# Routed experts on one core: the four with the fewest tokens in half the places, large and small alternating

## The chip, the core and the metric

One core of a Trainium2 chip runs the whole program: two blocks of a first kind, then two of a second. The time is device microseconds of that core, from launch to end; a profiled execution gives the span from the first to the last instruction. TensorE (PE) multiplies, VectorE (DVE) and ScalarE (ACT) work on SBUF and PSUM, SyncE (SP) issues the transfers. PEld is the loading of a stationary matrix into TensorE.

## The reference

The layer that the change touches routes each of 256 tokens of width 1024 to two of eight experts; the expert's inner width is 3584. The program computes the same sum, but each expert only over the tokens that chose it.

```python
def moe_swiglu(h, w_router, b_router, w_gate, w_up, w_down):
    t = h.reshape(B * S, D)
    logits = (t @ w_router).astype(jnp.float32) + b_router.astype(jnp.float32)
    top_v, top_i = lax.top_k(logits, TOP_K)
    top_w = jax.nn.softmax(top_v, axis=-1)
    gates = jnp.sum(jax.nn.one_hot(top_i, N_EXPERTS, dtype=jnp.float32) * top_w[..., None], axis=1)
    out = jnp.zeros_like(t)
    for e in range(N_EXPERTS):
        out = out + gates[:, e:e + 1].astype(t.dtype) * swiglu(t, w_gate[e], w_up[e], w_down[e])
    return out.reshape(B, S, D)
```

## The kernel before

All weights are float32 in memory and come in units of 128 x 2048 (1 MB), one transfer each, into four raw buffers. To multiply at float32 accuracy with TensorE's faster rounded type (float32r), every operand is cut into a high part, which is the value rounded, and a low part, which is what the rounding left. ScalarE makes the high part of a unit (`split_hi`, L549 to L553), VectorE the low part (`split_lo`, L1056 to L1059); each has three buffers. A product is then three matmuls: high by high, high by low, low by high (`mm3`, L1796, on L1789). SP loads a raw buffer again when the low part taken from it is done (`load`, L494 to L501), ScalarE writes a high buffer again when TensorE has used the unit in it. `take` on each engine moves this stream on by one unit; ScalarE and VectorE split two units ahead.

The router (L1463 on VectorE, L2216 on TensorE) computes the logits, marks for each token its two best experts (`rank`), counts on TensorE which place each token gets in its expert (`slots`), and the largest count (`most`). Every expert has 128 places. `routed` (L840, L1505, L2267) gathers the tokens of all experts with matmuls by one-hot matrices, four experts and one of eight pieces of the width in each of 16 steps. ScalarE copies the high rows out (`xghi`), VectorE the low ones (`xglo`). Between the router's steps TensorE runs matmuls of ones on nothing, so that it isn't idle (`keep_warm`, L1791).

An expert is cut into seven groups of 512 inner columns. A group is six units: two for gate, two for up (`up`, L2314 on TensorE, L854 on ScalarE, L1554 on VectorE) and two for down (`down`, L2335, L864, L1571). The tokens are the stationary operand, 512 weight columns move. A unit is 12 matmuls of 512 columns. After gate and up, ScalarE takes silu (L860), VectorE multiplies it by the up result and the token's gate (`mact`, L1565), TensorE turns the result round in four transposes (L2310), and the two engines split it again (`mahi`, `malo`, L882 and L1590). The 56 groups run expert by expert, `down` of a group behind `up` of the next. An expert's output stays in two PSUM banks over its seven groups, is split (`ohi`, `olo`), and goes back to the tokens by scatter matmuls in four pieces (`expert_to_x`, L2302), which VectorE adds to the residual stream `xT` (L1550). The order of the 336 units in memory and in time is `MOE_ORDER`, a constant.

If one expert has more than 128 tokens, a flag makes a second, unpipelined round run over all weights (`over_round`). In the profiled run it doesn't run.

Of the kernel before, what the change touches and what calls it, by code (L numbers as in the profile page):

```python
# [56 lines left out]
PER_G = 6  # L57
U_MOE = PER_G * NG
# [3 lines left out]
MOE_ORDER = [0, 1, 2, 3]  # L62
# [62 lines left out]
def build(nc, io):  # L125
    ctx = ExitStack()
    with ctx:
# [54 lines left out]
        half_out = sem("expert_half_out")  # L182
        lam_dotted, lam_exped = sem("lam_dotted"), sem("lam_exped")
# [45 lines left out]
        mahi_end = rt.put("mahi_end", [P, GF // P, P], F32R)  # L229
        malo_end = rt.put("malo_end", [P, GF // P, P], F32R)  # L230
# [6 lines left out]
        vx = base.put("vx", [P, 8 + 64 + 8 + 64])  # L237
# [6 lines left out]
        small = base.put("small", [P, 512])  # L244
        stat = base.put("stat", [P, PB, 8])
        overflow = base.put("overflow", [1, 1], mybir.dt.int32)
        rstd = base.put("rstd", [P, S])
# [15 lines left out]
        iota = c1.put("iota", [P, P])  # L263
        at_moe = c1.top + -c1.top % 256
# [70 lines left out]
        gs1 = rm.put("gs1", [P, 1])  # L335
        r = Region(at_places)
        ohi = r.put("ohi", [P, D], F32R)
        olo = r.put("olo", [P, D], F32R)
        rows_hi_T = at("rows_hi_T", [P, NT, D], at_hhi, F32R)
# [52 lines left out]
        def moe_act(n):  # L392
            return (mahi_end, malo_end) if n == NG - 1 else (mahi, malo)
# [99 lines left out]
        def sync_program(sp):  # L493
            def load(s):  # L494
# [15 lines left out]
            for name, t in (("onehot", onehot_in), ("lbw", lbw), ("ident", ident), ("bsum", bsum),  # L510
                            ("lmask", lmask), ("halves", halves), ("tri", tri), ("future", future_in), ("v2", v2), ("vx", vx),
                            ("iota", iota)):
                sp.dma_start(t[:], io[name]).then_inc(small_loaded, 16)
            for s in range(4, U_SECOND + RAW):
                load(s)
            sp.wait_ge(expert_added, 4 * NE)
            flag = sp.value_load(overflow[0:1, 0:1], min_val=0, max_val=1)
            with sp.If(flag > 0):
                for r in range(1, ROUNDS):
                    with sp.Fori(0, NE) as e:  # L520
                        for i in range(PER_G * GE):
                            n = (r - 1) * U_MOE + i
                            sp.wait_ge(over_used, e * (PER_G * GE) + (n + 1))
                            sp.dma_start(slow_raw[:], io["wm"][bass.ds(e * (PER_G * GE) + i, 1), :, :].rearrange(
# [11 lines left out]
        def scalar_program(act):  # L536
# [18 lines left out]
            def take():  # L555

                s = stream.next() - 1
                if s + LEAD < U_ALL:
                    split_hi(s + LEAD)
# [280 lines left out]
            def routed(r):  # L840
                for i in range(16):
                    es, k, b = slice(4 * (i // DK), 4 * (i // DK) + 4), i % DK, i % 4 * 2
                    after(gathered_hi)
                    act.activation(xghi[:, es, k, :], PS[:, b, :].rearrange("p (e s) -> p e s", e=4),
                                   ACT.Copy).then_inc(taken_act, 1)
                after(places_turned)
# [6 lines left out]
            def experts():  # L853
                def up(n):  # L854
                    take()
# [3 lines left out]
                    act.wait_ge(unit_used, used)  # L859
                    act.activation(msil[:], PS[:, 2 + 2 * (n % 2), :], ACT.Silu).then_inc(moe_silu, 1)  # L860
                    take()
                    take()

                def down(n):  # L864
                    take()
                    if n == NG - 1:
                        after(half_out)
                        act.activation(ohi[:, 0:512], PS[:, 0, :], ACT.Copy).then_inc(out_hi, 1)
                        act.wait_ge(unit_used, stream.n + 1)
                        act.activation(ohi[:, 512:], PS[:, 1, :], ACT.Copy).then_inc(out_hi, 1)  # L870
                        take()
                        return
                    if n == NG - 2:
                        turn(n + 1)
                    used = take()
                    if n % GE == GE - 1:
                        act.wait_ge(unit_used, used)
                        act.activation(ohi[:], banks(0, 2), ACT.Copy).then_inc(out_hi, 1)

                def turn(n):  # L880
                    after(moe_turned)
                    act.activation(moe_act(n)[0][:].rearrange("p f s -> p (f s)"), PS[:, 6, :],  # L882
                                   ACT.Copy).then_inc(moe_hi, 1)

                up(0)
                for n in range(1, NG):
                    up(n)
                    down(n - 1)
                    if n < NG - 1:
                        turn(n)  # L890
                down(NG - 1)
# [151 lines left out]
        def vector_program(dve):  # L1043
# [17 lines left out]
            def take():  # L1061

                s = stream.next() - 1
                if s + LEAD < U_ALL:
# [196 lines left out]
            def first_mixer(l):  # L1261
# [6 lines left out]
                if l == 0:  # L1268
                    after(small_loaded, 16 * 11)
                    dve.tensor_copy(future[:], future_in[:].unsqueeze(1).to_broadcast([P, 2, P]))  # L1270
                    dve.tensor_copy(ident_r[:], ident[:])
                    dve.memset(nd[:].bitcast(F32), 0.0)
# [188 lines left out]
            eq = small[:, 192:320].rearrange("p (t e j) -> p t e j", t=NT, e=NE)  # L1461

            def router():  # L1463
# [22 lines left out]
                token_rows(0)  # L1486
                after(slots_done)
                cnt = PS[:, 3, 0:NT * NE].rearrange("p (t e) -> p t e", t=NT)
                dve.tensor_tensor(slots.rearrange("p (t e) -> p t e", t=NT), cnt, rank, ALU.mult).then_inc(slots_shifted, 1)
                after(slots_shifted)  # L1490

            def gating():
# [5 lines left out]
                step(dve.tensor_tensor(ex, ex, m.unsqueeze(2).to_broadcast([P, NT, NE]), ALU.mult))  # L1498
                halves = idg[:, :, P:TG].rearrange("p t (e h) -> p t e h", h=2)
                step(dve.tensor_copy(halves[:, :, :, 0], ex))  # L1500
                dve.tensor_copy(idg[:, :, 0:P], ident[:].unsqueeze(1).to_broadcast([P, NT, P]))
                dve.tensor_tensor(halves[:, :, :, 1], ex, halves[:, :, :, 0].bitcast(F32),
                                  ALU.subtract).then_inc(gates_ready, 1)

            def routed(r):  # L1505
                sl = small[:, 416:432] if r else slots
                if r:
                    dve.tensor_scalar(sl, slots, float(-P * r), None, ALU.add).then_inc(slots_shifted, 1)
                    after(slots_shifted)

                def place(es):
                    shape = [P, NT, NE // 2, P]
                    slot_of = sl.rearrange("p (t e) -> p t e", t=NT)[:, :, es]
                    dve.tensor_tensor(places[:, :, es, :], iota[:].unsqueeze(1).unsqueeze(1).to_broadcast(shape),
# [3 lines left out]
                if r == 0:  # L1518
                    after(totals_done)
                    dve.tensor_reduce(most, PS[0:1, 1, 32:32 + NE], AX, ALU.max).then_inc(slots_ready, 1)  # L1520
                    after(slots_ready)
                    token_rows(1)
                for i in range(16):
# [24 lines left out]
            def expert_to_x(e, q, bank=None):  # L1548
                after(scattered)
                dve.tensor_tensor(pair(xT, q), pair(xT, q), PS[:, bank or 6 + q % 2, :],  # L1550
                                  ALU.add).then_inc(expert_added, 1)

            def experts():
                def up(n):  # L1554
                    e = n // GE
                    for i in range(4):
                        if n == 1 and i == 2:
                            turn(0)
                        if n % GE == 2 and n > GE and 1 <= i <= 2:
                            expert_to_x(e - 1, 1 + i)  # L1560
                        if n or i < 3:
                            used = take()
                    after(moe_silu)
                    dve.wait_ge(unit_used, used + (n == 0))
                    dve.scalar_tensor_tensor(out=mact[:], in0=msil[:], scalar=gsl[:, e:e + 1],  # L1565
                                             in1=PS[:, 3 + 2 * (n % 2), :], op0=ALU.mult,
                                             op1=ALU.mult).then_inc(moe_mult, 1)
# [3 lines left out]
                def down(n):  # L1571
                    take()
                    if n == NG - 2:
                        turn(n + 1)
                    if n < NG - 1:
                        take()
                    if n == NG - 1:
                        for c in range(2):
                            cs = slice(c * 512, (c + 1) * 512)
                            after(out_hi)  # L1580
                            dve.tensor_tensor(olo[:, cs], PS[:, c, :], ohi[:, cs].bitcast(F32),
                                              ALU.subtract).then_inc(out_lo, 1)
                    elif n % GE == GE - 1:
                        after(out_hi)
                        dve.tensor_tensor(olo[:], banks(0, 2), ohi[:].bitcast(F32), ALU.subtract).then_inc(out_lo, 1)

                def turn(n):
                    hi, lo = (x[:].rearrange("p f s -> p (f s)") for x in moe_act(n))
                    after(moe_hi)
                    dve.tensor_tensor(lo, PS[:, 6, :], hi.bitcast(F32), ALU.subtract).then_inc(moe_lo, 1)  # L1590

                up(0)
                for n in range(1, NG):
                    up(n)
                    if n % GE == 1 and n > 1:
                        expert_to_x(n // GE - 1, 0)
                        expert_to_x(n // GE - 1, 1)
                    down(n - 1)
                    if n < NG - 1:
                        turn(n)  # L1600
                down(NG - 1)
                for q in range(4):
                    expert_to_x(NE - 1, q, (6, 7, 2, 3)[q])
# [165 lines left out]
        def tensor_program(pe):  # L1769
# [314 lines left out]
            def first_mixer(l):  # L2084
# [3 lines left out]
                if l == 0:  # L2088
                    after(small_loaded, 16 * 11)
# [126 lines left out]
            def router():  # L2216
# [34 lines left out]
                keep_warm(0, 12)  # L2251
# [442 lines left out]
```

## Time and profile before

| | us |
|---|---|
| median of three runs | 2510.22 |
| lowest, highest | 2506.88, 2510.34 |
| the profiled execution: its own time | 2507.98 |
| the profiled execution: span | 2506.2 |
| expert stage, first to last expert matmul | 586.2 to 1566.0 |

In the rows below, times are us from the start of the span unless marked ns. In the table of stretches a row has the stretch and its length, then for each engine (PE, PEld, DVE, ACT, POOL) its busy time and, in brackets, its instructions; then come the granted TensorE clock as a share of 2.4 GHz, the busy share of the 16 transfer engines, and the rate. Matmul ends are modelled and matmuls overlap, so the step from one to the next counts, not the duration.

### The profile page before, as it was taken

How to read it: one execution, taken by the hardware profiler on the slowest of the kernel's cores; microseconds unless marked ns; L12 is line 12 of the kernel's file. 1: busy time of each engine (PE TensorE's matmuls, PEld its weight loads, DVE VectorE, ACT ScalarE, POOL GpSimd, SP SyncE). 2: the span in 40 equal slices, each digit the busy share in tenths (PEclk: the TensorE clock that was granted, in tenths of full speed). 3: DMA queues.
4: the chain of work that ended last, by engine and by line, in shares of the span. 5: the costliest groups of instructions: out<-in, count | busy, mean ns of one | idle time of the engine just before them, and what ended most of it. 6: DMA issues, size and time to landing. Idle time of an engine off the chain costs nothing.

```text
span 2506.2 us, 38463 instructions
## 1 busy us (share of the span) xinstructions
PE 2463.3 (98%) x16646; PEld 2220.8 (89%) x16646; DVE 1863.2 (74%) x1635; ACT 1520.1 (61%) x1558; POOL 0.2 (0%) x4
## 2 busy tenths in 40 slices
PE   9999999999999999999999999999999999999998
PEld 8899999887888888888888888998999999899998
DVE  6765557858888889888888888756875565767655
ACT  6563436567777777777777777557653365665433
POOL 0000000000000000000000000000000000000000
PEclk9999999999999999999999999999999999999999
DMA  6335554325999999999999999433444543343552
GB/s 250 135 120 185 184 187 150 135 85 207 369 350 366 357 365 359 363 361 365 353 359 353 368 356 367 168 135 118 152 166 175 198 167 138 118 168 135 186 185 85
DMA packets 83314, 585.25 MB, mean 234 GB/s; under 512 B 9245, under 2 KB 11133, under 8 KB 12613
## 3 DMA queue, kind: packets, MB, share of 16 engines
q1 hardware_dynamic: 83140, 582.73, 62.8%
q8 instruction: 135, 2.21, 0.4%
q14 instruction: 39, 0.31, 0.0%
HBM read 581.64 MB, written 1.05 MB: 232 GB/s over the span
## 4 chain that ended last, share of the span: by engine, by line
PE 85%; DVE 7%; ACT 4%; DMA 2%; issue 1%; DVEq 0%; SPq 0%; ACTq 0%
PE PS L1789 84%; DVE wlo L1058 3%; ACT whi L553 2%; DMA raw<-in_wm 2%; PE PS L2310 1%; PE PS L1993 1%; DVE stat L1190 0%; ACT pb L666 0%; DVE hT L1104 0%; ACT pt L681 0%; DVE lf L1244 0%; DVE pb L1215 0%; DMA xT<-in_xT 0%; DVE xT L1363 0%; DVE yT L1249 0%
## 5 line engine op out<-in xcount | busy, mean ns | idle before, releaser
L1058 DVE TENSOR_TENSOR wlo<-raw,whi 128x2048 fp32r<-128x2048 f32 x550 | 1257.9, 2291 | 376.3 <-ACT whi L553 368.5
L553 ACT ACTIVATE whi<-raw 128x2048 fp32r<-128x2048 f32 x550 | 1051.6, 1913 | 322.0 <-PE PS L1789 289.0
L1789 PE MATMUL PS<-hhi,whi 128*128 128x256 f32 x1984 | 569.7, 287 | 6.3 <-DVE wlo L1058 1.7
L1789 PE MATMUL PS<-hhi,wlo 128*128 128x256 f32 x1984 | 558.2, 281 | 0.0
L1789 PE MATMUL PS<-hlo,whi 128*128 128x256 f32 x1984 | 558.0, 281 | 0.0
L1789 PEld LDWEIGHTS PS<-hhi,whi 128*128 128x128 f32 x1984 | 373.4, 188 | 16.8 <-issue 12.0
L1789 PEld LDWEIGHTS PS<-hlo,whi 128*128 128x128 f32 x1984 | 373.6, 188 | 1.0 <-issue 0.5
L1789 PEld LDWEIGHTS PS<-hhi,wlo 128*128 128x128 f32 x1984 | 373.4, 188 | 0.0
L1789 PE MATMUL PS<-whi,xghi 128*128 128x512 f32 x896 | 358.9, 401 | 2.2 <-DVE wlo L1058 2.0
L1789 PE MATMUL PS<-whi,xglo 128*128 128x512 f32 x896 | 353.8, 395 | 0.0
L1789 PE MATMUL PS<-wlo,xghi 128*128 128x512 f32 x896 | 353.5, 395 | 0.0
L1789 PEld LDWEIGHTS PS<-whi,xghi 128*128 128x128 f32 x896 | 168.8, 188 | 41.4 <-DVE wlo L1058 5.0
L1789 PEld LDWEIGHTS PS<-whi,xglo 128*128 128x128 f32 x896 | 168.6, 188 | 39.6
L1789 PEld LDWEIGHTS PS<-wlo,xghi 128*128 128x128 f32 x896 | 169.0, 189 | 36.3
L1789 PE MATMUL PS<-whi,mahi 128*128 128x512 f32 x440 | 173.7, 395 | 0.3 <-DVE wlo L1058 0.3
L1789 PE MATMUL PS<-whi,malo 128*128 128x512 f32 x440 | 173.7, 395 | 0.0
L1789 PE MATMUL PS<-wlo,mahi 128*128 128x512 f32 x440 | 173.5, 394 | 0.0
L1789 PE MATMUL PS<-blo,whi 128*128 128x256 f32 x512 | 144.1, 281 | 0.0
L1789 PE MATMUL PS<-bhi,wlo 128*128 128x256 f32 x512 | 144.1, 281 | 0.0
L1789 PE MATMUL PS<-bhi,whi 128*128 128x256 f32 x512 | 144.1, 281 | 0.0
L1002 ACT ACTIVATE bhi<-rl 128x512 fp32r<-128x512 f32 x32 | 20.2, 633 | 155.6 <-DVE rl L1727 155.6
L1789 PEld LDWEIGHTS PS<-whi,mahi 128*128 128x128 f32 x440 | 82.9, 188 | 19.9 <-DVE wlo L1058 0.9
(364 smaller groups left out, 3540.8 us busy)
## 6 DMA issues: line engine op xcount, KB each, us to landing
raw<-in_wm SPq DMA_DIRECT2D x336, 1024.0 KB, 5.6
raw<-in_ws SPq DMA_DIRECT2D x214, 1024.0 KB, 4.8
xT<-in_xT SPq DMA_DIRECT2D x4, 256.0 KB, 7.8
bsum<-in_bsum SPq DMA_DIRECT2D x1, 1024.0 KB
out_T<-hT SPq DMA_DIRECT2D x4, 256.0 KB, 2.5
lmask<-in_lmask SPq DMA_DIRECT2D x1, 512.0 KB
onehot_in<-in_onehot SPq DMA_DIRECT2D x1, 288.0 KB
lbw<-in_lbw SPq DMA_DIRECT2D x1, 256.0 KB
```

The lines of the kernel that those rows point to most:

```text
L553: act.activation(whi[s % SPLIT][:], raw[s % RAW][:], ACT.Copy).then_inc(hi_ready, 1)
L1002: act.activation(bhi[i][:], rl[i][:].rearrange("p (t s) -> p t s", t=2), ACT.Copy).then_inc(ff_hi, 1)
L1058: dve.tensor_tensor(wlo[s % SPLIT][:], raw[s % RAW][:], whi[s % SPLIT][:].bitcast(F32), ALU.subtract).then_inc(lo_ready, 1)
L1789: return pe.matmul(out, a, b, start=start, stop=stop, skip_group_check=True)
L1993: ins = pe.transpose(tp[:, i, b, :], buf[:, head, b * P:(b + 1) * P], ident[:])
L2310: ins = pe.transpose(PS[:, 6, f * P:(f + 1) * P], mact[:, f * P:(f + 1) * P], ident[:])
```

## The change

The experts are ranked by their number of tokens on the chip. The places of experts, from most to least tokens, replace the expert numbers everywhere: `order` holds which expert stands at each place. SP waits for it (`order_ready`), reads it into registers and computes each expert weight's address from them.

The first four places keep 128 token places and three matmuls a product. The last four get 64. For them the high rows of the tokens fill columns 0 to 63 of the one stationary matrix and the low rows columns 64 to 127 (`packed`), so that two matmuls (by the high and by the low weights) make all products (`mm2`; the product of low by low, which the three matmuls leave out, comes along). The result has the high rows' share in partitions 0 to 63 and the low rows' in 64 to 127. ScalarE copies the lower half out (`low_half`), and a matmul with a shifted identity adds it to the upper (`folded`); silu, product, transposes and splits then run on 64 rows. The down product is packed in the same way (`mas`).

Groups of a large and a small expert alternate (`group`): 28 pairs. Gate and up have one PSUM bank each instead of two, outputs of a large expert stay in banks 0 and 1, of a small one in 4 and 5. Scatter pieces are spread over units by a table (`SCATTERS`). The first two units of the stage are split within the gather steps instead of ahead of them, and their transfers wait for the ranking. The second round now runs when a large expert has over 128 tokens or a small one over 64. The diff's core:

```diff
+NL = NE // 2
+HALF = P // 2
+
+
+def group(n):
+
+    q, side = n // 2, n % 2
+    return q // GE + NL * side, q % GE, side
+
+
+MOE_ORDER = [(0, i) for i in range(4)]
 for n in range(1, NG):
-    MOE_ORDER += [PER_G * n + i for i in range(4)] + [PER_G * (n - 1) + i for i in (4, 5)]
-MOE_ORDER += [PER_G * (NG - 1) + i for i in (4, 5)]
+    MOE_ORDER += [(n, i) for i in range(4)] + [(n - 1, i) for i in (4, 5)]
+MOE_ORDER += [(NG - 1, i) for i in (4, 5)]
+
+SCATTERS = {}
+for e in range(NL - 1):
+    n = 2 * GE * e
+    for q, at_unit in enumerate([(n + 14, 2), (n + 14, 4), (n + 15, 0), (n + 15, 2)]):
+        SCATTERS[at_unit] = (e, q)
+    for q, at_unit in enumerate([(n + 15, 4), (n + 16, 0), (n + 16, 2), (n + 16, 4)]):
+        SCATTERS[at_unit] = (e + NL, q)
...
+        def turned_act(n):
+
+            if n % 2 == 0:
+                flat4 = lambda t: t[:].rearrange("p f s -> p (f s)")
+                return PS[:, 6, :], flat4(mahi), flat4(malo)
+            return (PS[:, 6, 0:GF // 2].rearrange("p (f s) -> p f s", s=HALF), mas[:, :, 0:HALF], mas[:, :, HALF:P])
...
-                    src = io["wm"][MOE_ORDER[s - U_FIRST]]
+                    n, i = MOE_ORDER[s - U_FIRST]
+                    e, g, _ = group(n)
+                    if e not in chosen:
+                        chosen[e] = sp.value_load(order[0:1, e:e + 1], min_val=0, max_val=NE - 1)
+                    src = io["wm"][bass.ds(chosen[e] * U_EXPERT + (PER_G * g + i), 1), :, :].rearrange("a p n -> p (a n)")
...
+            for s in range(4, U_FIRST):
+                load(s)
+            sp.wait_ge(order_ready, 1)
+            for s in range(U_FIRST, U_SECOND + RAW):
...
+                    if r == 0 and i in (10, 13):
+                        split_hi(U_FIRST + (i > 10))
...
+                def low_half(bank, i):
+                    act.activation(lows[i][HALF:P, :], PS[HALF:P, bank, :], ACT.Copy).then_inc(lows_taken, 1)
+
+                def silu(rows_):
+                    act.activation(msil[0:rows_, :], PS[0:rows_, 2, :], ACT.Silu).then_inc(moe_silu, 1)
...
+                        low_half(2, 0)
...
+                    if n + 1 < NG and group(n + 1)[2]:
+                        act.wait_ge(unit_used, above)
+                        low_half(3, 1)
+                        after(gate_folded)
+                        silu(HALF)
...
+                dve.tensor_copy(by_expert[:, 0, :], vx[:, 152:160])
+                after(totals_done)
+                step(dve.tensor_copy(by_expert[:, 1, :], PS[:, 1, 32:32 + NE]))
+                mine = by_expert[:, 1, :].unsqueeze(2).to_broadcast([P, NE, NE])
+                other = by_expert[:, 1, :].unsqueeze(1).to_broadcast([P, NE, NE])
+                earlier = vx[:, 80:144].rearrange("p (e j) -> p e j", e=NE)
+                ahead, same = gt[:, 0], eq[:, 0]
+                dve.tensor_tensor(ahead, other, mine, ALU.is_gt)
+                step(dve.tensor_tensor(same, other, mine, ALU.is_equal))
+                step(dve.tensor_tensor(same, same, earlier, ALU.mult))
+                step(dve.tensor_tensor(ahead, ahead, same, ALU.add))
+                step(dve.tensor_reduce(place_of, ahead, AX, ALU.add))
                 after(slots_done)
                 cnt = PS[:, 3, 0:NT * NE].rearrange("p (t e) -> p t e", t=NT)
-                dve.tensor_tensor(slots.rearrange("p (t e) -> p t e", t=NT), cnt, rank, ALU.mult).then_inc(slots_shifted, 1)
+                dve.tensor_tensor(by_expert[:, 2:4, :], cnt, rank, ALU.mult).then_inc(slots_shifted, 1)
                 after(slots_shifted)
+                step(dve.tensor_tensor(holds, vx[:, 152:160].unsqueeze(2).to_broadcast([P, NE, NE]),
+                                       place_of.unsqueeze(1).to_broadcast([P, NE, NE]), ALU.is_equal))
+                to_places(by_place, by_expert, 4)
+                dve.tensor_copy(order[:], by_place[0:1, 0, :]).then_inc(order_ready, 1)
+
+            def to_places(dst, src, n):
+
+                moved = small[:, 512:512 + n * NE * NE].rearrange("p (a r e) -> p a r e", a=n, r=NE)
+                step(dve.tensor_tensor(moved, src.unsqueeze(2).to_broadcast([P, n, NE, NE]),
+                                       holds.unsqueeze(1).to_broadcast([P, n, NE, NE]), ALU.mult))
+                step(dve.tensor_reduce(dst, moved, AX, ALU.add))
...
+                to_places(ex_place, ex, NT)
...
+                    packed = r == 0 and i >= DK
+                    ss = slice(HALF if packed else 0, P)
                     after(gathered)
-                    dve.tensor_copy(xglo[:, es, k, :], PS[:, b, :].rearrange("p (e s) -> p e s",
-                                                                             e=4)).then_inc(taken_dve, 1)
+                    dve.tensor_copy((xghi if packed else xglo)[:, es, k, ss],
+                                    PS[:, b, :].rearrange("p (e s) -> p e s", e=4)[:, :, ss]).then_inc(taken_dve, 1)
+                    if r == 0 and i in (11, 15):
+                        split_lo(U_FIRST + (i > 11))
...
+                def mult(n, used=None):
+                    e, _, side = group(n)
+                    rows_ = HALF if side else P
+                    after(moe_silu)
+                    if side:
+                        after(up_folded)
+                    else:
+                        dve.wait_ge(unit_used, used)
+                    dve.scalar_tensor_tensor(out=mact[0:rows_, :], in0=msil[0:rows_, :], scalar=gsl[0:rows_, e:e + 1],
+                                             in1=PS[0:rows_, 3, :], op0=ALU.mult, op1=ALU.mult).then_inc(moe_mult, 1)
...
+                        mult(n + 1)
...
+                            expert_to_x(q, (7, 2, 3, 7)[q])
...
-                keep_warm(0, 6)
+                keep_warm(0, 30)
...
+                def folded(bank, i, sem):
+                    after(lows_taken)
+                    mm(PS[:, bank, :], fold[HALF:P, :], lows[i][HALF:P, :], False, True).then_inc(sem, 1)
+
+                def mm2(out, a, b_hi, b_lo, start, stop):
+                    mm(out, a, b_hi, start, False)
+                    return mm(out, a, b_lo, False, stop)
...
+                                ins = mm2(PS[:, b, :], xghi[:, e, kk, :], w_hi[:, cs], w_lo[:, cs], kk == 0, False)
+                            else:
+                                ins = mm3(PS[:, b, :], xghi[:, e, kk, :], xglo[:, e, kk, :], w_hi[:, cs], w_lo[:, cs],
+                                          kk == 0, kk == DK - 1)
...
+                        folded(2, 0, gate_folded)
...
+                        if i == 0 and n + 1 < NG and group(n + 1)[2]:
+                            folded(3, 1, up_folded)
...
+                    (turned_half if n % 2 else turned_rows)().then_inc(moe_turned, 1)
...
+                    expert_to_x(NL - 1, q, (7, 2, 3, 7)[q])
```

## Rows read from the trace of the kernel before

**Rows 1.** Stretch from:to, length, PE PEld DVE ACT POOL, clock, transfer share, GB/s.
```profile
586.20:1566.00 979.80, 977.50 (x4368) 793.39 (x4368) 859.02 (x492) 707.38 (x462) 0.00 (x0) 1.00 0.94 359
```
**Rows 2.** Chain of waits in the expert stage: start, us, what.
```profile
599.53 2.21 DVE wlo L1058
...
1491.31 0.44 PE PS L2310 x4
1491.74 16.74 PE PS L1789 x72
```
**Rows 3.** Chain of waits at the end of the expert stage.
```profile
1566.06 0.61 ACT ohi L870
...
1566.69 0.70 DVE olo L1581
...
1567.43 1.21 PE PS L1789 x8
1568.65 2.85 issue
```
**Rows 4.** Waits from 650 to 1500 us: total us, times, longest.
```profile
ACT whi L553 <- PE PS L1789: 111.5, 158, 1.8
...
ACT whi L553 <- DMA raw<-in_wm: 32.7, 32, 2.5
...
PEld PS L1789 <- DVE wlo L1058: 3.7, 10, 1.0
PE PS L1789 <- DVE wlo L1058: 1.2, 3, 0.5
```
**Rows 5.** Groups by shape, 650 to 1500 us: busy, mean ns, idle before.
```profile
L1058 DVE TENSOR_TENSOR wlo<-raw,whi 128x2048 fp32r<-128x2048 f32 x292 | 667.9, 2291 | 103.4 <-ACT whi L553 97.7
L553 ACT ACTIVATE whi<-raw 128x2048 fp32r<-128x2048 f32 x292 | 559.3, 1916 | 144.4 <-PE PS L1789 111.5 <-DMA raw<-in_wm 32.7
...
L1565 DVE SCALAR_TENSOR_TENSOR mact<-msil,small,PS 128x512 f32<-128x512 f32 x48 | 35.6, 741 | 0.0
L1590 DVE TENSOR_TENSOR malo<-PS,mahi 128x512 fp32r<-128x512 f32 x49 | 33.5, 683 | 0.0
...
L860 ACT ACTIVATE msil<-PS 128x512 f32<-128x512 f32 x49 | 29.3, 599 | 42.0 <-PE PS L1789 42.0
...
L1550 DVE TENSOR_TENSOR xT<-xT,PS 128x512 f32<-128x512 f32 x28 | 18.5, 679 | 0.0
...
L1585 DVE TENSOR_TENSOR olo<-PS,ohi 128x1024 fp32r<-128x1024 f32 x7 | 8.5, 1217 | 0.0
```
**Rows 6.** Stretches with full transfer engines; then the page's transfers of expert weights.
```profile
650.00:1500.00 850.00, 848.81 (x3805) 689.93 (x3804) 746.93 (x424) 612.49 (x397) 0.00 (x0) 1.00 0.95 360
...
604.00:608.00 4.00, 4.00 (x21) 3.28 (x20) 2.73 (x2) 2.69 (x3) 0.00 (x0) 1.00 0.99 410
...
1500.00:1510.00 10.00, 10.00 (x47) 8.15 (x46) 9.50 (x6) 6.80 (x5) 0.00 (x0) 1.00 0.99 384
1550.00:1560.00 10.00, 10.00 (x46) 8.14 (x46) 8.44 (x6) 7.44 (x5) 0.00 (x0) 1.00 0.99 399
...
raw<-in_wm SPq DMA_DIRECT2D x336, 1024.0 KB, 5.6
```
**Rows 7.** Chain of waits from the router to the first expert.
```profile
565.49 0.30 DVE small L1482
...
570.41 15.66 PE PS L1789 x76
...
589.57 0.54 DVEq L1754
```
**Rows 8.** Timeline of TensorE and of SP's queue.
```profile
562.81 2.94 PE L1789 MATMUL PS<-ones 128*128 128x128 f32 x24
...
503.19 195.49 SPq L501 DMA_DIRECT2D raw<-in_wm  x44
```
**Rows 9.** Table of stretches: behind the expert stage.
```profile
1566.00:1572.00 6.00, 2.95 (x19) 2.52 (x19) 4.83 (x10) 5.95 (x11) 0.00 (x0) 0.85 0.10 38
```

More of the change, by code:

```diff
@@ L519, in sync_program @@
                 for r in range(1, ROUNDS):
[L520 to L524, printed above, removed]
+                    for e in range(NE):
+                        one = sp.value_load(order[0:1, e:e + 1], min_val=0, max_val=NE - 1)
+                        for i in range(U_EXPERT):
+                            sp.wait_ge(over_used, (r - 1) * U_MOE + e * U_EXPERT + i + 1)
+                            sp.dma_start(slow_raw[:], io["wm"][bass.ds(one * U_EXPERT + i, 1), :, :].rearrange(
                                 "a p n -> p (a n)")).then_inc(over_landed, 16)
@@ L557, in take @@
                 s = stream.next() - 1
-                if s + LEAD < U_ALL:
+                if s + LEAD < U_ALL and s + LEAD not in (U_FIRST, U_FIRST + 1):
                     split_hi(s + LEAD)
@@ L858, in up @@
                         turn(0)
-                    act.wait_ge(unit_used, used)
-                    act.activation(msil[:], PS[:, 2 + 2 * (n % 2), :], ACT.Silu).then_inc(moe_silu, 1)
+                    if side == 0:
+                        act.wait_ge(unit_used, used)
+                        silu(P)
                     take()
-                    take()
-                def down(n):
-                    take()
+                    if side:
+                        act.wait_ge(unit_used, used)
+                        low_half(2, 0)
@@ L866, in down @@
+                    return take()
+                def down(n, above):
+                    e, g, side = group(n)
+                    o_hi = outs[side][0]
+                    take()
+                    if n + 1 < NG and group(n + 1)[2]:
[3 more added lines that the diff above has]
+                        silu(HALF)
                     if n == NG - 1:
                         after(half_out)
-                        act.activation(ohi[:, 0:512], PS[:, 0, :], ACT.Copy).then_inc(out_hi, 1)
+                        act.activation(o_hi[:, 0:512], PS[:, 4, :], ACT.Copy).then_inc(out_hi, 1)
@@ L885, in experts @@
                 up(0)
                 for n in range(1, NG):
[L887 to L891, printed above, removed]
+                    above = up(n)
+                    down(n - 1, above)
+                    turn(n)
+                down(NG - 1, None)
             def over_round(r):
@@ L1063, in take @@
                 s = stream.next() - 1
-                if s + LEAD < U_ALL:
+                if s + LEAD < U_ALL and s + LEAD not in (U_FIRST, U_FIRST + 1):
                     split_lo(s + LEAD)
@@ L1513, in place @@
                     slot_of = sl.rearrange("p (t e) -> p t e", t=NT)[:, :, es]
-                    dve.tensor_tensor(places[:, :, es, :], iota[:].unsqueeze(1).unsqueeze(1).to_broadcast(shape),
+                    numbers = iota2 if r == 0 and es.start else iota
+                    dve.tensor_tensor(places[:, :, es, :], numbers[:].unsqueeze(1).unsqueeze(1).to_broadcast(shape),
                                       slot_of.unsqueeze(3).to_broadcast(shape), ALU.is_equal).then_inc(places_ready, 1)
@@ L1518, in routed @@
                 if r == 0:
-                    after(totals_done)
-                    dve.tensor_reduce(most, PS[0:1, 1, 32:32 + NE], AX, ALU.max).then_inc(slots_ready, 1)
+                    step(dve.tensor_tensor(most_of, by_place[0:1, 1, :], vx[0:1, 144:152], ALU.mult))
+                    dve.tensor_reduce(most, most_of, AX, ALU.max).then_inc(slots_ready, 1)
                     after(slots_ready)
@@ L1558, in up @@
                             turn(0)
-                        if n % GE == 2 and n > GE and 1 <= i <= 2:
-                            expert_to_x(e - 1, 1 + i)
                         if n or i < 3:
                             used = take()
[L1563 to L1567, printed above, removed]
+                        if (n, i) in SCATTERS:
+                            expert_to_x(SCATTERS[n, i][1])
+                    if group(n)[2] == 0:
+                        mult(n, used + (n == 0))
                     if n == 0:
@@ L1571, in down @@
                 def down(n):
+                    e, g, side = group(n)
+                    o_hi, o_lo = outs[side]
                     take()
-                    if n == NG - 2:
-                        turn(n + 1)
+                    if (n + 1, 4) in SCATTERS:
+                        expert_to_x(SCATTERS[n + 1, 4][1])
+                    if n + 1 < NG and group(n + 1)[2]:
+                        mult(n + 1)
                     if n < NG - 1:
@@ L1577, in down @@
                     if n == NG - 1:
+                        for q in range(4):
+                            expert_to_x(q, (7, 2, 3, 7)[q])
                         for c in range(2):
@@ L2251, in router @@
                 keep_warm(0, 12)
+                claim(1)
                 claim(3)
                 after(rank_ready)
+                for t in range(NT):
+                    ins = mm(PS[:, 1, 32:32 + NE], ones[:], rank[:, t, :], t == 0, t == NT - 1)
+                ins.then_inc(totals_done, 1)
                 for t in range(NT):
@@ L2258, in router @@
                 empty(3, 1, slots_shifted)
-                claim(1)
-                for t in range(NT):
-                    ins = mm(PS[0:1, 1, 32:32 + NE], ones[:, 0:1], rank[:, t, :], t == 0, t == NT - 1)
-                ins.then_inc(totals_done, 1)
                 empty(1, 1, slots_ready)
-                keep_warm(0, 6)
+                keep_warm(0, 30)
                 pe.wait_ge(rows_hi, NT)
@@ L2292, in routed, with scatter @@
                     emptied[b] = (slot_gates_taken, taken)
-            def scatter(q, bank, at_places):
+            def scatter(q, bank, at_places, o_hi=ohi, o_lo=olo):
                 for f in range(2):
@@ L2297, in scatter, with expert_to_x, turned_half @@
                     out = PS[:, bank, f * S:(f + 1) * S]
[L2298 to L2303 removed]
+                    mm(out, o_hi[:, cs], at_places, True, False)
+                    ins = mm(out, o_lo[:, cs], at_places, False, True)
+                return ins
+            def expert_to_x(e, q, bank=7):
                 claim(bank)
[L2305 removed]
+                pe.wait_ge(out_lo, 2 * (e % NL) + e // NL + 1)
+                scatter(q, bank, pm[:, e, :], *outs[e // NL]).then_inc(scattered, 1)
                 empty(bank, 1, expert_added)
+            def turned_half():
+                for f in range(GF // P):
+                    ins = pe.transpose(PS[:, 6, f * HALF:(f + 1) * HALF], mact[0:HALF, f * P:(f + 1) * P],
+                                       ident[0:HALF, 0:HALF])
+                return ins
             def turned_rows():
@@ L2349, in down @@
                             cs = slice(f * D + c * 512, f * D + (c + 1) * 512)
-                            ins = mm3(PS[:, c, :], a_hi[:, 2 * i + f, :], a_lo[:, 2 * i + f, :], w_hi[:, cs],
-                                      w_lo[:, cs], n % GE == 0 and i == 0 and f == 0,
-                                      n % GE == GE - 1 and i == 1 and f == 1)
+                            ff, first, end = 2 * i + f, g == 0 and i == 0 and f == 0, g == GE - 1 and i == 1 and f == 1
+                            if side:
+                                ins = mm2(PS[:, acc + c, :], mas[:, ff, :], w_hi[:, cs], w_lo[:, cs], first, end)
+                            else:
+                                ins = mm3(PS[:, acc + c, :], mahi[:, ff, :], malo[:, ff, :], w_hi[:, cs], w_lo[:, cs],
+                                          first, end)
                             if last and f == 1 and c == 0:
@@ L2367, in experts @@
                     up(n)
-                    if n % GE == 1 and n > 1:
-                        pe.wait_ge(out_lo, C.now(out_lo))
-                        expert_to_x(n // GE - 1, 0)
-                        expert_to_x(n // GE - 1, 1)
                     down(n - 1)
-                    if n < NG - 1:
-                        turn(n)
+                    turn(n)
                 down(NG - 1)
-                pe.wait_ge(out_lo, C.now(out_lo))
+                for q in range(4):
+                    expert_to_x(NL - 1, q, (7, 2, 3, 7)[q])
                 for q in range(4):
```

131 lines of the change are left out of this document (71 added, 60 removed).

## The prediction

> **What bounds the kernel now.** I read the stage table first. The expert stage runs from 586.2 to 1566.0 us, 979.8 of the 2506.2 us span, with the weight transfers busy for 0.94 of it at 359 GB/s [rows 1]. So two resources look full there, TensorE and the transfers, and one has to find out which leads. The chain of waits names TensorE: in steady state it is nothing but 72 matmuls in 16.74 us and four transposes in 0.44 us, group after group [rows 2]. That is 0.2325 us a matmul, 2.79 us for a unit of 12, 17.18 us for a group of 6 units. 56 groups make 962.1 us; 28 scatter pieces at 0.6 us (two took 1.21 us, [rows 3]) make 16.9; that leaves about 1 us of stalls out of 979.8, so the sum closes. The list of waits agrees: in 850 us the matmuls waited 1.2 us and the weight loads 3.7 us for low parts, while ScalarE waited 111.5 us for TensorE to give buffers back, and only 32.7 us for a transfer [rows 4]. TensorE leads, but the next two are close. VectorE was busy 859.0 of 979.8 us [rows 1], and transfers are sometimes already last.
>
> **What one pair of groups costs after the change.** A pair is one large and one small group, 12 units; there are 28, and a pair now takes 979.8/28 = 35.0 us.
> - TensorE: the large group stays at 17.18. The small one drops every third matmul: 48 x 0.2325 = 11.16, plus two fold matmuls at 0.2325 each and half-width transposes (0.22 to 0.44, I take 0.3) = 11.9. With 32 scatter pieces over 28 pairs, 0.7: **29.8 us**. The removed 24 matmuls a pair are 5.6 us.
> - VectorE [rows 5]: twelve low parts at 2.29 = 27.5 (chained ones start 2.21 apart, [rows 2], which gives 26.5), two gate products 1.48, one full residual 0.68 and one of half the columns (0.34 to 0.68, I take 0.45), scatter adds 32 x 0.68 / 28 = 0.8, outputs 8 x 1.22 / 28 = 0.35: **30.3 to 31.3 us**. Nothing big left this engine.
> - ScalarE: 12 x 1.92 = 23.0; silu twice, two copies of the low half out of PSUM (not in the trace; priced as the 128x512 silu at 0.60), a full and a half residual: about 26 us. Not the bound.
> - Transfers: 12.58 MB a pair. At the 360 GB/s of today that is 34.95 us, but today TensorE sets the demand. Dividing by the busy share (0.95) gives 379 GB/s, 33.2 us. Stretches with the engines full moved 384 to 410 GB/s [rows 6], 32.8 to **30.7 us**.
>
> So three resources lie between 29.8 and 33.2. They don't overlap fully, since the work alternates with only four raw buffers and three split ones. In the large phase (six units in a row with three matmuls each) TensorE sets 2.79 a unit; in the small phase it needs 1.86 and waits for VectorE: six low parts 2.21 apart, a gate product and a residual. 16.8 + 0.7 of transposes + 13.3 + 1.4 = 32.2, with scatters 32.8. The transfers' mean gives 33.2 as the other limit. I take **33.0 us**. Stage: 28 x 33.0 + 1 = 925, against 979.8: **-54.8 us**.
>
> Waits that the change adds inside a pair. The up-half fold waits for ScalarE's copy, and VectorE's gate product waits for the fold, with the next low part queued behind it. It comes after the first down unit (2.79 us), while ScalarE needs 1.92 + 0.60 + 0.60 for the split, copy and silu queued there, and VectorE has a low part of 2.29 to do meanwhile; so I cost it at nothing. If TensorE runs ahead of that cover, some 0.5 us a pair. Gate and up banks are no longer doubled; a bank is claimed four units after it was read, so nothing. SP now reads an expert's number eight times and computes addresses from a register: the nearest row is VectorE's read of the flag, 0.54 us [rows 7]; no row shows such a load, so 0 to 1 us of latency each. A buffer's round trip (landing 5.6 [rows 6], split 1.92, low part 2.29, some 0.3 of hand-overs) is 10.1 us against 4 x 2.75 = 11.0, so I take nothing, with 0.3 us a pair at the upper end.
>
> **Before the experts.** Between the ranks and the first places VectorE gets 12 small steps of up to 0.30 us [rows 7], 3.0 us at 0.25. But the warming matmuls grow from 6 to 30: 12 of them are 24 records in 2.94 us [rows 8], so 30 take 7.35. They begin near 567.5 and now end near 574.8, later than the places. The first low-row gather, at 570.41 before [rows 7], follows one high round (0.9) later, at 575.7: **+5.3 us**, TensorE's warming being the last to end. Two high and two low splits (8.4 us in all) move into the gather. There the last eight copies shrink to half width on both engines, and a gather step is some 0.9 of the 15.66 us [rows 7], so that four banks of lead (3.6 us) cover one split: nothing, at worst +4. The first weight loads, issued from 503 us on before [rows 8], now wait for the order. SP has nothing else queued behind; four loads in 2.7 us each after the first landing are in by about 585, before ScalarE asks for the first at step 10. The fold constant, the extra 64 KB table and the extra columns of the gating step lie beside transfers and gathers: nothing.
>
> **After the last group.** Expert 3's four scatter pieces and adds come between the last down matmul and the last output. VectorE does four adds (4 x 0.68 = 2.7 us [rows 5], 0.4 more for their hand-overs) ahead of the residuals that now follow the evictions at once [rows 3]: +3.1. The last turn loses its early place: residuals 0.4 + 0.4 after the transposes, +1.1. **+4.2 us**, bounds 2 and 7.
>
> Sum: -54.8 + 5.3 + 4.2 = -45.3 against the profiled 2508.0 (span 2506.2 and 1.8 around it) gives 2462.7; the median of the runs, 2510.2, lies 2.2 higher: **2465 us**.
>
> **Rivals.**
> 1. The transfers can't go faster (slower by 14 us). If what the engines' 0.94 busy share moves is the ceiling, a pair takes 12.58 MB / 360 GB/s = 34.95, the stage saves 1 us at most and the 9.5 us at its ends remain; a little loss of continuity at each switch (0.2 a pair) makes it 2510 - 1 + 9.5 + 5 = 2524. It decides once the rate stays under 363 GB/s (34.65 a pair, where 28 x 0.34 pays for the 9.5). For it: 359 over the whole stage. Against it: 410 in 4 us, 384 and 399 in 10 us [rows 6]. The Trainium skill speaks for this rival ("DMA: Bandwidth & Descriptors", section "Where 436 GB/s comes from"): the memory side binds near 358 GB/s a core. By it the change gains nothing; the rows above exceed it for up to 10 us, no row shows it over a whole stage. Chance 0.11.
> 2. Register-addressed loads land late. With 2 us more each, a round trip of 12.1 us over four buffers is 3.0 a unit, 36.3 a pair: 2557; with 1 us 2.78, 33.3: 2473. Half of it inside my range. Chance outside 0.05.
> 3. TensorE's clock. Its small phase is idle for a third. The only drop in the stretch came after 2.85 us of waiting at the end of the stage: 0.85 granted over the 6 us around it [rows 3, 9]. At 1.2 GHz a small unit takes 3.7 us, +6 us a pair: 2630. The gaps I expect are 0.3 to 0.8 us. Chance 0.03.
> 4. It doesn't hold: an expert among the four smallest with more than 64 tokens sends all weights through the serial second round, 336 loads at 5.6 us, over 1.8 ms. The reference's router on its default inputs gives 50, 54, 58, 61, 61, 65, 77, 86: it fits. Chance 0.02.
> 5. Better: transfers at 400 GB/s and VectorE at 2.21 throughout, 31.7 a pair: 2429. Chance 0.07.
>
> **How the numbers follow.** My forecast keeps 0.72. Its own range is 32.2 to 34.1 a pair, 2443 to 2496. With the start and the end at their bounds and the better case let in, 2428 to 2500 leaves out about 0.2. A difference under 0.2% (5 us) can't be told from none. Faster: 0.72 + 0.07 + 0.01 of rival 2 = 0.80; same: 0.01 each of rivals 1 and 2 = 0.02; slower: the rest of rivals 1 to 4 = 0.18.
>
> **What would show it.** Right: in the expert stage TensorE waits for VectorE's low part in small groups, matmuls fall from 72 to 48 there, transfers exceed 370 GB/s over the stage, the granted clock stays 1.00, and the stage lasts about 925 us; gathers begin some 5 us later. Wrong: 360 GB/s again with ScalarE waiting for landings (rival 1), landings over 7 us with idle transfer engines (2), clock below 1 (3).

## The result and the profile after

The changed kernel takes 2527.4 us (median of three runs, 2522.7 to 2529.6) against 2510.2: ratio 1.0073, interval 1.005 to 1.0095. It is 0.7% slower, where I forecast 2465. The profiled execution took 2522.7 us with a span of 2520.9, 14.7 longer than before.

The table of stretches of the kernel after, the expert stage from its first expert matmul to its last down matmul (which ends at 1576.6), then the scatter behind it (columns as in [rows 1]):

```profile
590.90:1577.00 986.10, 898.99 (x3741) 668.18 (x3742) 847.08 (x487) 734.81 (x519) 0.00 (x0) 0.99 0.95 358
1577.00:1584.00 7.00, 4.65 (x29) 4.16 (x27) 6.28 (x10) 4.22 (x8) 0.00 (x0) 0.79 0.03 5
```

The stage is no shorter: 986 us against 979.8, at 358 GB/s against 359 [rows 1]. TensorE has 627 matmul records fewer and 87 us without a matmul on record, where it had 2.3. The rest lies at the two ends: the stage begins 4.7 us later (590.9 against 586.2), and its scatter ends at 1583.4, 6.8 us after the last down matmul instead of 2.6. The waits from 700 to 1500 us (total us, times, longest) of the kernel after:

```profile
DVE wlo L1118 <- ACT whi L595: 97.9, 137, 1.8
ACT whi L595 <- DMA raw<-in_wm: 90.7, 109, 2.2
PEld PS L1897 <- DVE wlo L1118: 78.9, 108, 2.4
ACT whi L595 <- PE PS L1897: 49.2, 67, 2.1
PE PS L1897 <- DVE wlo L1118: 39.5, 66, 1.9
```

Before, the splits on ScalarE waited 103.6 us for TensorE and 32.7 for transfers in this stretch ([rows 4] has a longer one); now they wait 49.2 and 90.7. TensorE's matmuls wait 39.5 us for low parts instead of 1.2, and its weight loads, part of whose waits pass while matmuls still run, 78.9 instead of 3.7. The page gives the landings:

```profile
raw<-in_wm SPq DMA_DIRECT2D x336, 1024.0 KB, 6.7
```

6.7 us from issue to landing instead of 5.6 [rows 6]. And the chain of waits, of which TensorE's matmuls were 86% in this stretch, now runs round raw buffers for much of its way: 29% matmuls, 25% transfers, 23% low and 11% high parts of weights. One lap of it in the kernel after:

```profile
945.53 0.05 SPq L540
...
945.68 6.69 DMA raw<-in_wm
...
952.39 1.92 ACT whi L595
...
954.34 2.29 DVE wlo L1118
956.63 0.60 DVE malo L1702
957.23 2.21 DVE wlo L1118
...
959.46 0.05 SPq L540
```

A buffer is loaded (6.69 us), its high part is made (1.92), then it stands while VectorE makes another unit's low part and an activation residual, then its own low part is taken and SP issues the next load into it: 13.9 us for one lap, in which four buffers take four units. It is a slow one: over the stage a unit takes 986/336 = 2.93 us, and four take 11.7.

### The profile page after: what moved, and what is told of

Its sections match the earlier page's. It is cut to its first block, busy times and chain, and to the rows that moved or that the text cites. A ratio compares the mean times of both kernels' runs of the same rounds, so it can differ in the third digit from the quotient of the medians.

```text
span 2520.9 us, 38121 instructions
## 1 busy us (share of the span) xinstructions
PE 2391.5 (95%) x16078; PEld 2102.9 (83%) x16078; DVE 1855.9 (74%) x1651; ACT 1544.9 (61%) x1614; POOL 0.2 (0%) x4
## 4 chain that ended last, share of the span: by engine, by line
PE 63%; DVE 15%; DMA 10%; ACT 9%; issue 3%; SPq 0%; DVEq 0%; ACTq 0%
PE PS L1897 61%; DMA raw<-in_wm 10%; DVE wlo L1118 10%; ACT whi L595 6%; PE PS L2101 1%; ACT up_lows L900 1%; DVE malo L1702 0%; DVE xT L1650 0%; DVE mact L1661 0%; DVE stat L1250 0%; ACT pb L708 0%; PE PS L2418 0%; DVE hT L1164 0%; ACT pt L723 0%; DVE lf L1304 0%
## 5 line engine op out<-in xcount | busy, mean ns | idle before, releaser
L1897 PE MATMUL PS<-whi,xghi 128*128 128x512 f32 x896 | 367.5, 410 | 47.6 <-DVE wlo L1118 45.9
L1897 PEld LDWEIGHTS PS<-wlo,xghi 128*128 128x128 f32 x896 | 169.1, 189 | 33.2
L1897 PE MATMUL PS<-whi,xglo 128*128 128x512 f32 x448 | 176.8, 395 | 0.0
L1897 PE MATMUL PS<-whi,mahi 128*128 128x512 f32 x224 | 97.1, 434 | 6.2 <-DVE wlo L1118 6.1
L1897 PEld LDWEIGHTS PS<-whi,xglo 128*128 128x128 f32 x448 | 84.4, 188 | 19.8
L708 ACT ACTIVATE pb<-PS,stat 128x256 f32<-128x256 f32 (+1 forms) x160 | 72.0, 466 | 40.0 <-DVE stat L1250 40.0
L1897 PEld LDWEIGHTS PS<-bhi,wlo 128*128 128x128 f32 x512 | 96.4, 188 | 0.0
L1897 PEld LDWEIGHTS PS<-bhi,whi 128*128 128x128 f32 x512 | 96.4, 188 | 0.0
```

The costliest lines, as they stand in the source:

```text
L708: ins = act.activation(pb[:, i, 0:w], sp[:, i // 2, i % 2, 0:w], ACT.Exp, bias=m[:, i:i + 1], accum_out=z[:, i:i + 1])
L1897: return pe.matmul(out, a, b, start=start, stop=stop, skip_group_check=True)
```

## The experiments

Two theories for the 358 GB/s. **Ceiling:** the path from memory carries no more, rival 1 of the prediction. **Round trip:** it carries more, but four raw buffers, held through both splits, keep it from being asked.

**x1, transfers alone.** No kernel of the program: SP loads the expert units and waits for the load that many places back.

```python
PHASES = [(1, 30), (2, 60), (3, 60), (4, 60), (8, 60)]
...
            for depth, n in PHASES:
                for i in range(n):
                    if i >= depth:
                        arrived(sp, s - depth)
...
                    sp.dma_start(raw[s % RING][:], io["wm"][s]).then_inc(landed[s % RING], 16)
```

> Only transfers of expert weight units (1 MB each, into a ring of eight buffers, nothing computed; the output is the input x), in phases: 30 units one at a time, then 60 each with two, three, four and eight outstanding. Ceiling theory (the path from memory carries no more than about 360 GB/s): from two or three outstanding on, every phase runs at 355 to 370 GB/s, 2.83 to 2.95 us a unit, and eight outstanding gain nothing. Round-trip theory (the path carries more; in the kernel four buffers, which are held through both splits, keep it from being filled): two outstanding give 340 to 370, eight give 380 to 425 GB/s, 2.47 to 2.76 us a unit.

One stretch inside each phase, with one, two, three, four and eight outstanding (stretch, length, POOL, clock, busy share of the transfer engines, GB/s):

```profile
10.00:140.00 130.00, 0.00 (x0) 1.00 0.61 218
160.00:290.00 130.00, 0.00 (x0) 1.00 0.99 395
320.00:440.00 120.00, 0.00 (x0) 1.00 1.01 422
480.00:600.00 120.00, 0.00 (x0) 1.00 1.01 422
640.00:750.00 110.00, 0.00 (x0) 1.00 1.01 422
```

The ceiling theory falls: 395 GB/s with two outstanding, more than the round-trip theory had expected of two, and 422 from three on, 2.48 us a unit. The Trainium skill's figure of 358 GB/s ("DMA: Bandwidth & Descriptors", section "Where 436 GB/s comes from") isn't what held this kernel; the measurement decides.

**x2 and x4, half the bytes,** in the kernel after and in the kernel before.

```diff
+                if U_FIRST <= s < U_SECOND:
+                    sp.dma_start(raw[s % RAW][:, 0:UNIT // 2], src[:, 0:UNIT // 2]).then_inc(raw_landed[s % RAW], 16)
+                    return
                 sp.dma_start(raw[s % RAW][:], src).then_inc(raw_landed[s % RAW], 16)
```

> The changed kernel, but of each expert unit only the first half of the columns is loaded (the other half of the buffer keeps old values), so results of the experts are left out. Both theories hold transfers for the bound: the expert stage falls from 986 us to what the engines need, 32.2 to 32.8 us a pair, 900 to 920 us, the total to 2440 to 2460 us. If the coupling of the engines were the bound and not the transfers, the stage would stay above 970 us.

> The kernel before, with the first half of each expert unit loaded, the experts' results left out in the same way. If TensorE bounds it, as the prediction had it: stage 975 to 980 us, total 2500 to 2510 us. If transfers already held it as much as TensorE, it gains more than 10 us.

2465.3 us and 2508.3 us, one execution each. The kernel after gains some 62 us when its transfers are halved, the kernel before nothing (its span is 2506.3 us at half the bytes, 2506.2 at all). The kernel before from 586 to 1566 us, with half the bytes:

```profile
586.00:1566.00 980.00, 978.52 (x4385) 795.75 (x4384) 861.57 (x496) 709.74 (x465) 0.00 (x0) 1.00 0.55 182
```

So TensorE did bound the kernel before, and what transfers cost the kernel after is the whole of my missing gain. The run of the kernel after misses its expected ranges, though: the total by 5 us, and the stage lasts 931 us instead of 900 to 920, so the engines alone need 33.2 us a pair and not 32.2 to 32.8. Its chain of waits shows what is left, one pair of groups:

```profile
899.74 0.74 DVE mact L1664
900.48 4.41 DVE wlo L1121 x2
904.88 0.60 DVE malo L1705
905.48 4.41 DVE wlo L1121 x2
...
909.94 8.97 PE PS L1900 x34
918.91 0.39 PE PS L2421 x4
919.30 8.58 PE PS L1900 x36
...
932.12 0.74 DVE mact L1664
```

32.4 us from one gate product to that of the next pair, VectorE in the small phase and TensorE in the large one by turns.

**x3 and x5, six and five raw buffers** in the expert stage.

```diff
+EXTRA = 6
...
+    b = (s - U_FIRST) % EXTRA if U_FIRST <= s < U_SECOND else s % RAW
+    PREV.append(max([p for p in range(s) if RING[p] == b], default=None))
...
-        xglo = rm.put("xglo", [P, NE, DK, P], F32R)
+        xglo = rm.put("xglo", [P, NL, DK, P], F32R)
+        rm.to(256, 128)
+        raw += [rm.put(f"raw{i}", [P, UNIT]) for i in range(RAW, EXTRA)]
...
-                if s >= RAW:
-                    sp.wait_ge(lo_ready, s - RAW + 1)
+                if PREV[s] is not None:
+                    sp.wait_ge(lo_ready, PREV[s] + 1)
```

> The changed kernel with six raw buffers in the expert stage instead of four (in the room of the low rows that packed experts don't use; the second round, which doesn't run with these inputs, is left out). Ceiling theory: no change, 2520 to 2532 us, landings grow to 9 us or more as more of them queue. Round-trip theory: the transfer engines' busy share goes from 0.95 to 0.99 or more and a unit takes 2.65 to 2.80 us, the stage 895 to 945 us, the total 2440 to 2485 us.

> The changed kernel with five raw buffers in the expert stage (the second round left out). If the buffers' round trip of 11.5 us over four buffers was the bound, five give 2.3 us a unit, under what the engines need, and most of the gain of six is there: 2463 to 2480 us. If six buffers gained by smoothing long disturbances, five give about half of it, 2490 to 2500 us.

Six: 2463.7 us (2463.0 to 2464.3), 0.983 of the kernel before (0.9813 to 0.9846). Five: 2468.9 (2465.6 to 2475.9), 0.9853 (0.9829 to 0.9876). The stretch from 650 to 1500 us with four, five and six buffers, as three kernels' tables have it:

```profile
650.00:1500.00 850.00, 779.40 (x3250) 579.49 (x3251) 734.78 (x418) 633.99 (x445) 0.00 (x0) 0.99 0.95 360
```
```profile
650.00:1500.00 850.00, 814.07 (x3426) 609.08 (x3425) 766.75 (x440) 667.54 (x467) 0.00 (x0) 0.99 0.98 379
```
```profile
650.00:1500.00 850.00, 816.11 (x3443) 610.43 (x3443) 768.65 (x443) 671.91 (x468) 0.00 (x0) 1.00 0.98 381
```

360, 379, 381 GB/s, and 3250, 3426, 3443 matmuls done in the same time. ScalarE's waits from 700 to 1500 us with six buffers, and the landings:

```profile
ACT whi L607 <- PE PS L1909: 94.6, 171, 3.9
ACT mas L956 <- PE PS L2430: 38.2, 21, 1.8
ACT msil L915 <- PE PS L1909: 19.3, 24, 0.8
ACT mahi L956 <- PE PS L2436: 6.8, 21, 0.4
ACT ohi L951 <- PE PS L1909: 4.3, 3, 1.4
```
```profile
raw<-in_wm SPq DMA_DIRECT2D x336, 1024.0 KB, 7.2
```

The wait for transfers, 90.7 us with four buffers and 15.2 with five, has left the list, and the stage is as long as with half the bytes (931 us): transfers cost nothing any more. And this though a single load takes longer, 7.2 us instead of 6.7: on average 2.6 are under way from 650 to 1500 us, where four buffers had 2.2. The transfer engines' busy share of 0.98 is a little under the 0.99 that I had expected. One buffer more than four is nearly enough. The time follows the number of buffers until the engines bind, as the round-trip theory has it.

**x6 and x7, the third matmul back** in small groups, with four buffers and with six.

```diff
                     mm(out, a, b_hi, start, False)
-                    return mm(out, a, b_lo, False, stop)
+                    mm(out, a, b_lo, False, False)
+                    return mm(out, a, b_hi, False, stop)
```

> The changed kernel, four buffers, but every product of a small group gets a third matmul again (the high part a second time, which changes the experts' results), so TensorE does as much work as before the change. If the round trip of the buffers sets the time, the matmuls taken away are worth little here: 2527 to 2550 us. If TensorE's work still told, 24 matmuls of 0.2325 us in 28 pairs come on top: 2527 + 156 = 2680 us at most.

> Six buffers and the third matmul in small groups together (the experts' results changed, the second round left out). With the buffers out of the way TensorE is the bound again: 17.18 + 17.18 + 0.47 + 0.7 and some 0.5 of waits a pair, 36.0 us, the stage 1009 us: 2535 to 2555 us, 70 to 90 us above the same kernel with two matmuls. If two matmuls instead of three are worth nothing, it stays at 2464 us.

2555.0 us (2553.2 to 2556.7) and 2553.4 us (2549.7 to 2554.6); the first is 5 us over its expected range. With TensorE the bound again (95% and 98% of the chain from 650 to 1500 us are its matmuls) the number of buffers makes no difference. The same matmuls taken away are worth 2555.0 - 2527.4 = 28 us with four buffers and 2553.4 - 2463.7 = 90 us with six. And this prices the rest of the change: alternation, folds, ranking and ends together cost 47 to 49 us against the kernel before (ratios 1.0189 and 1.0195), which has to be earned first.

**x8, constant addresses.**

```diff
-                    if e not in chosen:
-                        chosen[e] = sp.value_load(order[0:1, e:e + 1], min_val=0, max_val=NE - 1)
-                    src = io["wm"][bass.ds(chosen[e] * U_EXPERT + (PER_G * g + i), 1), :, :].rearrange("a p n -> p (a n)")
+                    src = io["wm"][[2, 0, 6, 3, 5, 1, 7, 4][e] * U_EXPERT + (PER_G * g + i)]
```

> The changed kernel with four buffers, but SP takes the experts' weights at constant addresses in the order that the ranking gives for these inputs, with no reads of the order and no address from a register; it still waits for the ranking. If register addresses cost nothing in the loop, as the prediction had it: 2520 to 2532 us. If each load starts 0.1 to 0.3 us later for them, the loop of four buffers shortens by that, 0.03 to 0.08 us a unit: 2500 to 2518 us.

2522.8 us, but from 2513.9 to 2533.9: the runs spread too far to see a few us. Its profiled execution, the slowest of them, shows the same picture, landings of 7.0 us and 355 GB/s. Register addresses aren't the cause of the missing 62 us; a cost of some 10 us stays open. In the lap above SP takes 0.15 us from the low part to the issue.

**x9 and x10, a kernel faster than both.** Six buffers with the second round kept, the two extra ones on top of low rows that only that round uses (it doesn't run with these inputs, so no run shows the two together); then with fewer warming matmuls as well.

```diff
+        free = rm.top + NL * DK * P * 4
         xglo = rm.put("xglo", [P, NE, DK, P], F32R)
+        raw += [at(f"raw{i}", [P, UNIT], free + (i - RAW) * UNIT * 4) for i in range(RAW, EXTRA)]
...
-                keep_warm(0, 30)
+                keep_warm(0, 20)
```

> The changed kernel with six raw buffers in the expert stage and the second round kept: the two extra buffers share the memory of the low rows that packed experts only need in the second round. As with six buffers without the second round: 2460 to 2468 us, ratio to the kernel before 0.981 to 0.985. If the second round's code or the shared memory cost anything, it is above 2470.

> The same with 20 warming matmuls ahead of the gather instead of 30. The low rows are ready at 573.1 us in the trace of the changed kernel, and the warming ends at 574.8: ten fewer end it at 572.4, so the gather starts about 1.7 us earlier and the total falls by 1 to 2 us, 2459 to 2466 us. If the gather's start doesn't reach the end of the program (the first weights land later than it needs them), nothing changes.

2466.6 us, 0.9839 (0.9825 to 0.9852), and 2462.2 us, 0.9822 (0.9809 to 0.9836): 1.6% and 1.8% under the kernel before. x9 has the code that x3 and x5 leave out, so their gain doesn't come from leaving it out. The first expert matmul of the two, in their timelines of TensorE:

```profile
590.91 0.47 PE L1908 MATMUL PS<-whi,xghi 128*128 128x512 f32 x1
```
```profile
589.16 0.47 PE L1908 MATMUL PS<-whi,xghi 128*128 128x512 f32 x1 [0.17 <-issue]
```

The warming that outlasts its purpose cost 1.75 us at that point. In the trace of the kernel after it ends at 574.4 and not at 574.8, as the expectation has it, 1.3 us behind the low rows. The medians differ by 4.5 us, more than either; the intervals of the two overlap, so I claim no more than the 1.75.

## Why the prediction was wrong

**The step that failed** is the term for the buffer's round trip: "landing 5.6 [rows 6], split 1.92, low part 2.29, some 0.3 of hand-overs", 10.1 us "against 4 x 2.75 = 11.0, so I take nothing, with 0.3 us a pair at the upper end". I took the landing from the kernel before, and the two splits as if each began at once. Measured, the landing is 6.7 us, and with a unit every 2.93 us the four buffers' round is 11.7, which leaves some 5.0 for the rest instead of 4.5. In the lap shown the rest is 7.1 us, since VectorE serves another unit and a residual first. The 0.9 us of slack that I counted was gone, and a unit took 2.93 us: 35.2 us a pair instead of 33.0, 28 x 2.2 = 62 us, about what half the bytes give back. The round of 11.7 is no proof by itself: four buffers that are loaded again at once always go round in four units' time, also in the kernel before, which took 2.92 us a unit because of TensorE. That the buffers set the pace of the kernel after is shown by x3 and x5.

**Rival 1 had the right time** (2524) **for the wrong reason.** It said that 360 GB/s is a ceiling, and the rate did stay there, with ScalarE waiting for landings, the sign that I had given for it. The ring of buffers gives the same sign. But x1 moves 422, and the six-buffer kernel 381 over 850 us. A rate that stays put under two different loads isn't yet a limit of the path: the busy share adds up the time that packets took, and at 0.95 the kernel after still had 60 us to win; 0.98 went with 381 GB/s and 1.01 with 422.

**What held.** TensorE bounded the kernel before (x4). The stage with six buffers is 590.9 to 1521.5, 931 us, where I had 925. That this is so near is partly luck: I took 33.0 us a pair from between the engines' 32.2 to 32.8 and the transfers' mean of 33.2, but with six buffers transfers don't bind, and it is the engines that need 33.2. The fold's wait, which I took as nothing, isn't in the list of waits with six buffers. The first low-row gather came 4.8 us later where the sum had 5.3, set by the warming matmuls (x10); the end +4.2 by the sum, and 4.2. Rival 3 (the clock) can hold little of it: in the stage the granted clock was at its lower level, 1.2 GHz, for 24 of 986 us with four buffers and 10 of 931 with six, so at most some 7 of the 62 us are its price. Rival 4 didn't happen.

**What stays open.** Why loads take longer to land at an unchanged rate is in part in the traces. From 650 to 1500 us both kernels move 360 GB/s, but in the kernel before 143 of 291 loads were issued while two others were under way, in the kernel after 219 of 290. Such loads landed in 6.6 and 6.8 us (medians), those that found one other in 4.9 and 5.3. So the loads of the kernel after come more in bursts. The rest is open: one, two and three loads were under way for 5, 70 and 25% of that time, and at the rates that x1 shows for them this would be some 393 GB/s (an estimate), where 360 were moved. No run separates the other engines' use of SBUF from other causes.

## What to carry to other kernels

When one engine's work is cut, price the ring that feeds it at the new pace, buffer by buffer: landing under the new demand plus the time the consumers really hold a buffer, queueing included, over the number of buffers. An average rate or a busy share near one says neither that the path is full nor that it has room; a stream of the same transfers alone tells it at once. And a cut that leaves memory idle (here the low rows) can pay for the buffer that it needs.

## What was not expected

Two 1 MB loads outstanding already give 94% of what three or more reach (395 and 422 GB/s), while one at a time gives 218. And with TensorE no longer the bound, the granted clock dipped a little: 0.99 over the stage, and 0.79 in the 7 us of scatter after it, where TensorE works 4.65 us.
